# Shared expert and router of one tile in products of 256 and 320 columns, with the last projection half split around the turn

## The chip, the cores and the metric

The kernel runs on one core of one Trainium2 chip. The metric is the device time of one execution in microseconds (us); lower is better. The kernel before takes 2959.06 us, the median of three runs (2958.59 to 2960.01). TensorE is called PE in the profile, its weight loads PEld, VectorE DVE, ScalarE ACT, GpSimd POOL and SyncE, which here only issues DMAs, SP.

## The reference

One encoder layer is applied to two sequences of 1024 rows of 1024 values, in 32-bit floats. The change lies in the part that joins the end of the first sub-layer to the beginning of the second. Cut to that part, the reference is:

```python
def encoder_layer(x, c, p):
    ...                                             # u, gate1, shift2, scale2, gate2 from x and c
    # mixer(u): merged = [rms_norm(att) | rms_norm(lru)]; merged @ w_out   (1024 -> 1024)
    x = ln_affine(DN_ALPHA * x + gate1 * mixer(u, p), p['ln1_g'], p['ln1_b'])
    u = ln_plain(x) * (1.0 + scale2) + shift2
    x = ln_affine(DN_ALPHA * x + gate2 * moe(u, p), p['ln2_g'], p['ln2_b'])
    return x

def moe(u, p):
    scores = jax.nn.sigmoid(xt @ p['w_router'])     # 1024 -> 64
    ...                                             # group-limited choice of 6 of 64 experts
    routed = routed_experts(xt, idx, w, p['w_exp_in'], p['w_exp_out'])
    shared = swiglu(xt, p['w_sh_in'], p['w_sh_out'])
    return (routed + shared).reshape(B, S, D)

def swiglu(x, w_in, w_out):
    g, up = jnp.split(x @ w_in, 2, axis=-1)         # 1024 -> 2 * 256
    return (jax.nn.silu(g) * up) @ w_out            # 256 -> 1024
```

## The kernel before

The program is a row of stages: `front` (input projection, recurrence), `attention`, `mixing`, `experts`, `output`. The change is in `mixing`, which is the stage from about 987 to 1470 us of the profiled span. It works on 16 tiles of 128 rows, numbered 0 to 15; tiles 0 to 7 are the first sequence (`KT` = 8), 8 to 15 the second. Nothing schedules it: every engine has its own hand-written program, its instructions run in the order of the code, and the engines meet at semaphores.

On PE, round `i` of the loop does the projection of tile `i` and the shared expert and router of tile `i - 1`:

- `project(pL, ...)`, both halves: the recurrence's part of `w_out` for tile `i`, 8 products of 512 columns (L1434).
- `turn(i)`: waits for `u2_ready`, the normalised rows of tile `i - 1`, and transposes them, 8 products of 128 columns (L1443). ACT copies them to `uT` (L1215).
- `project(pA, ..., 0)`, the first half of the attention's part of `w_out`, 4 products of 512 columns (L1434).
- `shared_in(i)`, gate and up columns of the shared expert, 8 products of 512 columns into `pH` (L1453).
- `project(pA, ..., 1)`, the second half, 4 products of 512 columns (L1434). Its end raises `pa_mm`.
- `gated(i)`: waits for `h_ready`, transposes the 256 gated values, 2 products (L1459).
- `logits`: the router's 64 columns, 8 products of 64 columns into `pB` (L1464).
- `shared_out(i)`: 4 products of 512 columns (L1472), then `rank` (L1481, L1482), 2 products of 64 columns.

A 32-bit product is two instructions in the trace, each with its own weight load: 8 products are "x16". Such an instruction is called a pass below.

On DVE, round `i` is: `add_lru(i)` (L1255, waits for `pl_mm`); `gate(i - 1)` (L1313, waits for ACT's silu of the gate columns, L1221); `add_att(i)` (L1261, waits for `pa_mm`); `norms(i)`, which is two layer norms, `add_shared(i - 1)` (L1267) among them and L1309 as its last instruction, which raises `u2_ready`; then `ranks(i - 2)` and `router(i - 1)`, a chain of some 30 small instructions. Tile 7 has more: before `gate(6)` and after `norms(7)` DVE folds the second sequence's gate into `w_out` (`fold`, L1282, 4 + 4 instructions), whose chunks come by DMA. PE's second projection of tile 8 waits for the last of them. Rounds 0 and 2 fold the shared expert's output weights (L1274) behind `norms`.

After round 15 PE turns tile 15, makes its logits first and its shared expert after them. DVE then has ranks, router and tables left, and its list of slots is what `experts` starts from.

Of the kernel before, what the change touches and what calls it, by code (L numbers as in the profile page):

```python
# [19 lines left out]
P = 128  # L20
# [1006 lines left out]
def mixing(nc, x, mod_d, w_out, weights, shared, keep, qx, lruT, u2_d, route, left, exp_weights, apart):  # L1027
# [9 lines left out]
    with ExitStack() as ctx:  # L1037
# [3 lines left out]
        wr, wsi, wso = sb("mx_wr", [P, KD, N_EXP]), sb("mx_wsi", [P, KD, 2 * D_E]), sb("mx_wso", [P, NB, D_E // P, D])  # L1041
# [43 lines left out]
        LOG, RNK = 0, 64  # L1085
# [7 lines left out]
        ut_mm, ut_copied, h_mm, silu_ready, h_ready, ht_mm, ht_copied = (sem("ut_mm"), sem("ut_copied"), sem("h_mm"), sem("silu_ready"), sem("h_ready"),  # L1093
# [8 lines left out]
        def _(sp):  # L1102
# [15 lines left out]
            sp.dma_start(wsi[:], w_sh_in.rearrange("(k p) f -> p k f", p=P)).then_inc(w_in, 16)  # L1118
# [4 lines left out]
            for dst, src in ((wr[:], w_router), (rb[:], router_bias.partition_broadcast(P)), (iota[:], iota_d.partition_broadcast(P))):  # L1123
                sp.dma_start(dst, src).then_inc(r_in, 16)
# [81 lines left out]
        def _(act):  # L1206
# [4 lines left out]
            def turned(i):  # L1211
                act.wait_ge(ut_mm, i)
                if i > 1:
                    act.wait_ge(log_mm, i - 1)
                nc.scalar.activation(uT, pU[:].rearrange("p a (k t) -> p (a k) t", t=P), ACT.Copy).then_inc(ut_copied, 1)  # L1215

            def shared_expert(i):
                act.wait_ge(h_mm, i)
                if i > 1:
                    act.wait_ge(h_ready, i - 1)  # L1220
                nc.scalar.activation(sl[:], pH[:, 0:D_E], ACT.Silu).then_inc(silu_ready, 1)  # L1221
                act.wait_ge(ht_mm, i)
# [4 lines left out]
            def scores(i, logits):  # L1227
                act.wait_ge(log_mm, i)
# [6 lines left out]
            for i in range(1, NT):  # L1235
                turned(i)
                shared_expert(i)
                scores(i, pB[:, LOG:LOG + N_EXP])
            turned(NT)
            scores(NT, pL[:, 0, 0:N_EXP])  # L1240
            shared_expert(NT)

        @block.vector
        def _(dve):
# [66 lines left out]
            def gate(i):  # L1311
                dve.wait_ge(silu_ready, i + 1)
                nc.vector.tensor_tensor(hg[:], sl[:], pH[:, D_E:2 * D_E], ALU.mult).then_inc(h_ready, 1)  # L1313
# [115 lines left out]
        def _(pe):  # L1429
            ident, tri, ones = cst[:, 0, :], cst[:, 1, :], cst[:, 2, :]  # L1430

            def project(out, which, src, i, h):
                for j in range(GQ):
# [12 lines left out]
            def shared_in(i):  # L1446
                if i > 1:
                    pe.wait_ge(ht_copied, i - 1)
                else:
                    pe.wait_ge(w_in, 48)  # L1450
                    pe.wait_ge(r_in, 48)
                for k in range(KD):
                    m = nc.tensor.matmul(pH[:], uT[:, k, :], wsi[:, k, :], start=(k == 0), stop=(k == KD - 1))  # L1453
# [8 lines left out]
            def logits(out):  # L1462
                for k in range(KD):
                    m = nc.tensor.matmul(out, uT[:, k, :], wr[:, k, :], start=(k == 0), stop=(k == KD - 1))  # L1464
# [11 lines left out]

# [7 lines left out]
            for i in range(NT):  # L1484
# [15 lines left out]
                project(pA, 0, attT, i, 1).then_inc(pa_mm, 1)  # L1500
                if i:
                    gated(i)
                    if i > 1:
                        pe.wait_ge(ez_ready, i - 1)
                    if i > 2:
                        pe.wait_ge(slots_ready, i - 2)
# [441 lines left out]
```

## Time and profile before

| | before |
|---|---|
| time, median of 3 runs | 2959.06 us (2958.59 to 2960.01) |
| profiled execution, its own time | 2960.4 us |
| its span, from the first to the last instruction | 2958.8 us |
| PE busy | 2760.2 us, 93% of the span |
| DVE busy | 1585.5 us, 54% |
| mean granted clock of PE | 0.969 |
| tile 6 to tile 7 in `mixing`, from turn to turn | 27.36 us |

An engine's busy time over the whole span is a mean over stages with different limits. What the change touches is read in the stage itself, from the rows of one tile in order of time and from the waits written behind them: a bracket such as [2.60 <-PE mx_pA L1434] says that the engine stood idle for 2.60 us just before the instruction, and that a PE instruction of line 1434 ended the wait. Products overlap in time, so the time that one takes is read from the start of one group of them to the start of the next, not from the duration in the row, which holds the last one's way through the array as well.

### The profile page before, as it was taken

The page shows a single profiled execution, that of the slowest core. Times are in us where ns is not written, and L with a number is a line of the kernel's source. Part 1 is how long each engine was busy: PE and PEld are TensorE (multiplying, and loading weights), DVE is VectorE, ACT ScalarE, POOL GpSimd, SP SyncE. Part 2 cuts the span into 40 slices and gives each one's busy share as a digit, 9 for nine tenths or more (in the row PEclk, how much of TensorE's full clock was granted, in tenths as well). Part 3 has the DMA queues.
Part 4 walks back from the last instruction along what each step waited for, and adds up shares of the span by engine and source line. Part 5 has one row for each costly group of instructions (what it writes and reads, how often), then busy time and mean ns, then how long its engine had stood idle before and what let it go on. Part 6 is the DMA issues. An engine that isn't in the chain of part 4 may idle for free. (4 is left out here: it accounts for less than half of the span.)

```text
span 2958.8 us, 31489 instructions
## 1 busy us (share of the span) xinstructions
PE 2760.2 (93%) x9160; PEld 1327.9 (45%) x9160; DVE 1585.5 (54%) x2549; ACT 698.0 (24%) x1222; POOL 1107.1 (37%) x1150
## 2 busy tenths in 40 slices
PE   6999999899999899899679999999999999999990
PEld 3345445455555345455334444444444444444440
DVE  3477357678877377777723333333333333333335
ACT  2354354366666111111100000000000000000005
POOL 2002001100000123223446665666665666665664
PEclk9999999999999999999889999999999999999995
DMA  8531000400000311211268798986978778989646
GB/s 330 188 112 54 18 32 8 160 12 12 9 11 8 140 65 65 100 59 49 79 212 252 203 325 235 310 255 166 289 207 265 212 227 248 281 285 307 162 99 255
DMA packets 189533, 466.46 MB, mean 158 GB/s; under 512 B 22282, under 2 KB 47050, under 8 KB 188042
## 3 DMA queue, kind: packets, MB, share of 16 engines
q1 hardware_dynamic: 137770, 311.89, 29.3%
q0 software_dynamic: 51680, 153.50, 21.2%
q8 instruction: 47, 0.77, 0.1%
q14 instruction: 36, 0.29, 0.0%
HBM read 361.38 MB, written 99.75 MB: 156 GB/s over the span
## 5 line engine op out<-in xcount | busy, mean ns | idle before, releaser
L1754 PE MATMUL ex_pH<-ring,ex_xT 128*128 x2096 | 945.4, 594 | 4.9 <-DVE ex_xT L1671 2.8
L1612 POOL DMA_INDIRECT kT<-s_u,ex_gidx x532 | 599.6, 1127 | 163.8 <-issue 159.8
L1754 PEld LDWEIGHTS ex_pH<-ring,ex_xT 128*128 128x128 f32 x2096 | 388.8, 191 | 446.5 <-issue 446.5
L1771 PE MATMUL ex_pY<-qT,ex_hT 128*128 x1040 | 467.6, 592 | 0.0
L1671 DVE STREAM_TRANSPOSE ex_xT<-kT 128x1024 f32<-128x1024 f32 x132 | 164.1, 1243 | 343.1 <-DMA kT<-s_u,ex_gidx 342.8
L1771 PEld LDWEIGHTS ex_pY<-qT,ex_hT 128*128 128x128 f32 x1040 | 197.5, 190 | 248.9 <-issue 248.9
L1632 POOL DMA_INDIRECT s_acc<-ex_y,ex_sidx x130 | 211.9, 1630 | 186.7 <-DVE ex_y L1706 121.7
L1706 DVE SCALAR_TENSOR_TENSOR ex_y<-ex_pY,ex_wgt,ex_G 128x1024 f32<-128x1024 f32 x130 | 166.9, 1284 | 183.3 <-PE ex_pY L1771 158.8
L1660 ACT ACTIVATE ex_hT<-ex_pG 128x256 f32<-128x256 f32 x130 | 50.0, 384 | 870.5 <-PE ex_pG L1741 857.1
L638 PE MATMUL fr_pF<-fr_uT,fr_wf 128*128 128x512 f32 x512 | 225.0, 595 | 1.3 <-ACT fr_uT L332 1.0
L1675 DVE TENSOR_TENSOR ex_h<-ex_silu,ex_pH 128x256 f32<-128x256 f32 x131 | 54.9, 419 | 318.7 <-ACT ex_silu L1651 318.5
L1701 DVE SCALAR_TENSOR_TENSOR ex_G<-mx_mrow,ex_second 128x1024 f32<-128x1024 f32 x130 | 166.7, 1282 | 0.0
L879 DVE TENSOR_REDUCE at_top<-at_pS 128x1 f32<-128x1024 f32 x128 | 155.8, 1217 | 16.1 <-PE at_pS L961 16.0
L827 POOL TENSOR_TENSOR mx_rms<-at_var,at_half 128x32 f32<-128x32 f32 x1 | 5.4, 5428 | 422.1 <-DVE at_var L944 422.1
L836 ACT ACTIVATE at_pr<-at_pS,at_nm,head_rms 128x1024 f32<-128x1024 f32 x128 | 153.8, 1202 | 21.0 <-DVE at_nm L880 21.0
L638 PEld LDWEIGHTS fr_pF<-fr_uT,fr_wf 128*128 128x128 f32 x512 | 96.1, 190 | 121.5 <-issue 121.2
L961 PE MATMUL at_pS<-kT,qT 64*128 64x512 f32 x256 | 146.1, 652 | 2.3 <-PEq L728 2.3
L1651 ACT ACTIVATE ex_silu<-ex_pH 128x256 f32<-128x256 f32 x131 | 50.4, 384 | 411.1 <-PE ex_pH L1754 408.1
L961 PE MATMUL at_pS<-kT,qx 64*128 64x512 f32 x256 | 146.1, 652 | 0.0
L970 PE MATMUL at_pX<-mx_cst,at_pr 128*128 128x128 f32 x1024 | 138.5, 279 | 3.8 <-ACT at_pr L836 3.1
L984 PE MATMUL at_pO<-at_pT,v 128*64 128x256 f32 x1024 | 138.5, 392 | 0.6 <-DVE qT L902 0.6
L1188 POOL DMA_INDIRECT s_list<-mx_entry,mx_slots x96 | 94.8, 988 | 112.9 <-DVE mx_slots L1366 88.5
(284 smaller groups left out, 3172.9 us busy)
## 6 DMA issues: line engine op xcount, KB each, us to landing
ring<-in_w_exp_in SPq DMA_DIRECT2D x64, 2048.0 KB
qT<-in_w_exp_out SPq DMA_DIRECT2D x64, 1024.0 KB
fr_wq<-in_w_ada SPq DMA_DIRECT2D x32, 512.0 KB, 5.5
kT<-s_u,ex_gidx POOLq DMA_INDIRECT x536
fr_wf<-in_w_in SPq DMA_DIRECT2D x16, 512.0 KB, 5.7
mx_x<-in_x SPq DMA_DIRECT2D x16, 512.0 KB
s_u<-v SPq DMA_DIRECT2D x16, 512.0 KB, 2.8
s_acc<-mx_x SPq DMA_DIRECT2D x16, 512.0 KB, 2.7
```

Of the source, the lines that this page charges most:

```text
L638: m = nc.tensor.matmul(pF[:, u % 2, :], wf[:, n % 4, k, :], uT[:, k, h * 512:(h + 1) * 512], start=(k == 0), stop=(k == KD - 1))
L836: nc.scalar.activation(pr[:, n % 2, :], pS[:, n % 2, :], ACT.Exp, bias=nm[:, n % 16:n % 16 + 1], scale=head_rms(n), accum_out=rs[:, n % 16 ...
L879: step(nc.vector.tensor_reduce(top[:, n % 16:n % 16 + 1], pS[:, n % 2, :], AX.X, ALU.max, negate=True))
L961: m = nc.tensor.matmul(pS[:, n % 2, h * 512:(h + 1) * 512], q, kT[rows, b, g, :], start=True, stop=True)
L970: m = nc.tensor.transpose(pX[:, h, k * P:(k + 1) * P], pr[:, n % 2, (4 * h + k) * P:(4 * h + k + 1) * P], ident)
L1612: nc.gpsimd.indirect_dma_start(xg[:, u, g, :], None, u2_q, bass.IndirectOffsetOnAxis(ap=gidx[:, u, g:g + 1].bitcast(U32), axis=0)).then_in ...
L1632: nc.gpsimd.indirect_dma_start(acc_d, bass.IndirectOffsetOnAxis(ap=sidx[:, u:u + 1].bitcast(U32), axis=0), y[:, u, :], None, compute_op=AL ...
L1671: nc.vector.transpose(xT[:, u, :, :].rearrange("p k (g j) -> p g k j", g=4), xg[:, u, :, :].rearrange("p g (k i) -> p g k i", i=S)).then_i ...
L1701: nc.vector.scalar_tensor_tensor(G[:], g2[:, 1, :], second[:, bass.ds(b, 1)], g2[:, 0, :], ALU.mult, ALU.add).then_inc(gate_ready, 1)
L1706: nc.vector.scalar_tensor_tensor(y[:, u, :], pY[:].rearrange("p a f -> p (a f)"), wgt[:, bass.ds(b, 1)], G[:], ALU.mult, ALU.mult).then_in ...
L1754: m = nc.tensor.matmul(pH[:], xT[:, u, k, :], wi[:, bass.ds(slot, 1), k, :].rearrange("p a f -> p (a f)"), start=(k == 0), stop=(k == KD - 1))
L1771: m = nc.tensor.matmul(pY[:, h, :], hT[:, c, :], wo[:, bass.ds(slot, 1), c, h * 512:(h + 1) * 512].rearrange("p a d -> p (a d)"), start=(c ...
```

## The change

The router's 64 columns are stored behind the shared expert's 512, in one tile `mx_wsi` of 576 columns. In rounds 1 to 15 `shared_in` now makes two groups: 8 products of 256 columns (the gate columns, into `pH`, raising the new semaphore `hs_mm`), then 8 products of 320 columns (up columns and router columns together, into `pB`, raising `h_mm`). ACT's silu waits for `hs_mm`, DVE's gate now for `h_mm` as well, and reads the up columns from `pB`. The separate products of 64 columns are gone in these rounds; the last tile keeps the old form. The second projection half is cut in two: 2 products, then `gated`, then 2 products, and `pa_mm` comes behind the last.

```diff
@@ -1038,7 +1038,7 @@
         sb = lambda n, s, d=F32: ctx.enter_context(nc.sbuf_tensor(n, s, d))
         ps = lambda n, s: ctx.enter_context(nc.psum_tensor(n, s, F32))
         sem = lambda n: ctx.enter_context(nc.semaphore("mx_" + n))
-        wr, wsi, wso = sb("mx_wr", [P, KD, N_EXP]), sb("mx_wsi", [P, KD, 2 * D_E]), sb("mx_wso", [P, NB, D_E // P, D])
+        wsi, wso = sb("mx_wsi", [P, KD, 2 * D_E + N_EXP]), sb("mx_wso", [P, NB, D_E // P, D])
         rb, ln, iota, tokf = sb("mx_rb", [P, N_EXP]), sb("mx_ln", [P, 2, D]), sb("mx_iota", [P, N_EXP]), sb("mx_tokf", [P, 1])
 
         attT, stg, ut = keep[0], keep[1][:].rearrange("p b g t -> p b (g t)"), keep[2][:].rearrange("p (s n) d -> p s (n d)", s=2)
@@ -1082,7 +1082,8 @@
         pH = ps("mx_pH", [P, 512])
         pB = ps("mx_pB", [P, 512])
         R1, R2, V1, V2 = range(4)
-        LOG, RNK = 0, 64
+
+        UP, LOG, RNK = 0, D_E, D_E + N_EXP
 
         once, x_in, stg_in, wo_folded = sem("once"), [sem(f"x_in{s}") for s in range(NX)], [sem("stg_in0"), sem("stg_in1")], sem("wo_folded")
         grow_in, tokf_in, ln_in, w_in, r_in = sem("grow_in"), sem("tokf_in"), sem("ln_in"), sem("w_in"), sem("r_in")
@@ -1090,7 +1091,7 @@
         var1, rstd1, x1_ready, z_stored, var2, rstd2, u2_ready, u2_stored = (
             sem("var1"), sem("rstd1"), sem("x1_ready"), [sem(f"z_stored{s}") for s in range(NX)], sem("var2"), sem("rstd2"), sem("u2_ready"),
             [sem("u2_stored0"), sem("u2_stored1")])
-        ut_mm, ut_copied, h_mm, silu_ready, h_ready, ht_mm, ht_copied = (sem("ut_mm"), sem("ut_copied"), sem("h_mm"), sem("silu_ready"), sem("h_ready"),
+        ut_mm, ut_copied, hs_mm, h_mm, silu_ready, h_ready, ht_mm, ht_copied = (sem("ut_mm"), sem("ut_copied"), sem("hs_mm"), sem("h_mm"), sem("silu_ready"), sem("h_ready"),
                                                                         sem("ht_mm"), sem("ht_copied"))
         log_mm, ez_ready, y_mm, z_ready, g2_in, wso_folded = sem("log_mm"), sem("ez_ready"), sem("y_mm"), sem("z_ready"), sem("g2_in"), sem("wso_folded")
         m_ready, rank_mm, slots_ready, listed = sem("m_ready"), sem("rank_mm"), sem("slots_ready"), [sem("listed0"), sem("listed1")]
@@ -1115,12 +1116,12 @@
             load_x(0)
             sp.dma_start(ln[:], ln1_rows.partition_broadcast(P)).then_inc(ln_in, 16)
             load_x(1)
-            sp.dma_start(wsi[:], w_sh_in.rearrange("(k p) f -> p k f", p=P)).then_inc(w_in, 16)
+            sp.dma_start(wsi[:, :, 0:2 * D_E], w_sh_in.rearrange("(k p) f -> p k f", p=P)).then_inc(w_in, 16)
             gate2 = lambda b: mod_d[b:b + 1, 5 * D:6 * D].partition_broadcast(P)
             for b in range(NB):
                 sp.dma_start(wso[:, b, :, :], w_sh_out.rearrange("(c p) d -> p c d", p=P)).then_inc(w_in, 16)
             sp.dma_start(g2[:], gate2(0)).then_inc(g2_in, 16)
-            for dst, src in ((wr[:], w_router), (rb[:], router_bias.partition_broadcast(P)), (iota[:], iota_d.partition_broadcast(P))):
+            for dst, src in ((wsi[:, :, 2 * D_E:], w_router), (rb[:], router_bias.partition_broadcast(P)), (iota[:], iota_d.partition_broadcast(P))):
                 sp.dma_start(dst, src).then_inc(r_in, 16)
             load_x(2)
             sp.dma_start(grow[:], mod_d[1:2, 2 * D:3 * D].partition_broadcast(P)).then_inc(grow_in, 16)
@@ -1211,21 +1212,26 @@
             def turned(i):
                 act.wait_ge(ut_mm, i)
                 if i > 1:
-                    act.wait_ge(log_mm, i - 1)
+                    act.wait_ge(h_mm, i - 1)
                 nc.scalar.activation(uT, pU[:].rearrange("p a (k t) -> p (a k) t", t=P), ACT.Copy).then_inc(ut_copied, 1)
 
-            def shared_expert(i):
-                act.wait_ge(h_mm, i)
+            def silu(i):
+                act.wait_ge(hs_mm, i)
                 if i > 1:
                     act.wait_ge(h_ready, i - 1)
                 nc.scalar.activation(sl[:], pH[:, 0:D_E], ACT.Silu).then_inc(silu_ready, 1)
+
+            def gated_rows(i):
                 act.wait_ge(ht_mm, i)
                 if i > 1:
                     act.wait_ge(y_mm, i - 1)
                 nc.scalar.activation(hT[:], pH[:, 0:FC * P].rearrange("p (c t) -> p c t", t=P), ACT.Copy).then_inc(ht_copied, 1)
 
             def scores(i, logits):
-                act.wait_ge(log_mm, i)
+                if i < NT:
+                    act.wait_ge(h_mm, i)
+                else:
+                    act.wait_ge(log_mm, 1)
                 if i > 2:
                     act.wait_ge(m_ready, i - 2)
                 nc.scalar.activation(ez[:, i % 2, :], logits, ACT.Exp, scale=-1.0).then_inc(ez_ready, 1)
@@ -1234,11 +1240,13 @@
             silu_table()
             for i in range(1, NT):
                 turned(i)
-                shared_expert(i)
+                silu(i)
+                gated_rows(i)
                 scores(i, pB[:, LOG:LOG + N_EXP])
             turned(NT)
             scores(NT, pL[:, 0, 0:N_EXP])
-            shared_expert(NT)
+            silu(NT)
+            gated_rows(NT)
 
         @block.vector
         def _(dve):
@@ -1310,7 +1318,12 @@
 
             def gate(i):
                 dve.wait_ge(silu_ready, i + 1)
-                nc.vector.tensor_tensor(hg[:], sl[:], pH[:, D_E:2 * D_E], ALU.mult).then_inc(h_ready, 1)
+
+                up = pH[:, D_E:2 * D_E]
+                if i < NT - 1:
+                    dve.wait_ge(h_mm, i + 1)
+                    up = pB[:, UP:UP + D_E]
+                nc.vector.tensor_tensor(hg[:], sl[:], up, ALU.mult).then_inc(h_ready, 1)
 
             def router(i):
                 by_rank = lambda a, n: a.unsqueeze(1).to_broadcast([P, n, a.shape[1]])
@@ -1429,8 +1442,8 @@
         def _(pe):
             ident, tri, ones = cst[:, 0, :], cst[:, 1, :], cst[:, 2, :]
 
-            def project(out, which, src, i, h):
-                for j in range(GQ):
+            def project(out, which, src, i, h, j0=0, j1=GQ):
+                for j in range(j0, j1):
                     m = nc.tensor.matmul(out[:, h, :], src[:, j, i * P:(i + 1) * P], wo[:, which, j, h * 512:(h + 1) * 512],
                                          start=(j == 0), stop=(j == GQ - 1))
                 return m
@@ -1449,8 +1462,20 @@
                 else:
                     pe.wait_ge(w_in, 48)
                     pe.wait_ge(r_in, 48)
+                first = D_E if i < NT else 2 * D_E
                 for k in range(KD):
-                    m = nc.tensor.matmul(pH[:], uT[:, k, :], wsi[:, k, :], start=(k == 0), stop=(k == KD - 1))
+                    m = nc.tensor.matmul(pH[:, 0:first], uT[:, k, :], wsi[:, k, 0:first], start=(k == 0), stop=(k == KD - 1))
+                m.then_inc(hs_mm, 1)
+                if i == NT:
+                    return
+
+                if i > 1:
+                    pe.wait_ge(ez_ready, i - 1)
+                    pe.wait_ge(h_ready, i - 1)
+                if i > 2:
+                    pe.wait_ge(slots_ready, i - 2)
+                for k in range(KD):
+                    m = nc.tensor.matmul(pB[:, 0:D_E + N_EXP], uT[:, k, :], wsi[:, k, D_E:], start=(k == 0), stop=(k == KD - 1))
                 m.then_inc(h_mm, 1)
 
             def gated(i):
@@ -1461,7 +1486,7 @@
 
             def logits(out):
                 for k in range(KD):
-                    m = nc.tensor.matmul(out, uT[:, k, :], wr[:, k, :], start=(k == 0), stop=(k == KD - 1))
+                    m = nc.tensor.matmul(out, uT[:, k, :], wsi[:, k, 2 * D_E:], start=(k == 0), stop=(k == KD - 1))
                 m.then_inc(log_mm, 1)
 
             def shared_out(i):
@@ -1473,7 +1498,6 @@
                 m.then_inc(y_mm, 1)
 
             def rank(i, read):
-
                 pe.wait_ge(m_ready, i)
                 pe.wait_ge(ez_ready, read)
                 if i > 1:
@@ -1497,14 +1521,11 @@
                 if i:
                     pe.wait_ge(ut_copied, i)
                     shared_in(i)
-                project(pA, 0, attT, i, 1).then_inc(pa_mm, 1)
+                project(pA, 0, attT, i, 1, 0, GQ // 2)
                 if i:
                     gated(i)
-                    if i > 1:
-                        pe.wait_ge(ez_ready, i - 1)
-                    if i > 2:
-                        pe.wait_ge(slots_ready, i - 2)
-                    logits(pB[:, LOG:LOG + N_EXP])
+                project(pA, 0, attT, i, 1, GQ // 2, GQ).then_inc(pa_mm, 1)
+                if i:
                     shared_out(i)
                 if i >= 2:
                     rank(i - 1, i)
```

PE's rows in one whole round of the loop before, which is alike in rounds 3 to 15: `mx_pL` and `mx_pA` are the two projections, `mx_pU` is first the turn and then the shared expert's output, `mx_pH` the shared expert's input columns and then the turned gated values, `mx_pB` the logits and the ranks.

```order
L1434 MATMUL mx_pL<-ring 128x512 x8
L1443 MATMUL mx_pU<-mx_cst,v 128x128 x8
L1434 MATMUL mx_pA<-ring,qT 128x512 x4
L1453 MATMUL mx_pH<-mx_wsi,qx 128x512 x8
L1434 MATMUL mx_pA<-ring,qT 128x512 x4
L1459 MATMUL mx_pH<-mx_cst,mx_h 128x128 x2
L1464 MATMUL mx_pB<-mx_wr,qx 128x64 x8
L1472 MATMUL mx_pU<-mx_wso,mx_hT 128x512 x4
L1481 MATMUL mx_pB<-mx_M,mx_cst 128x64
L1482 MATMUL mx_pB<-mx_Msum,mx_cst 128x64
```

The same round now:

```order
L1447 MATMUL mx_pL<-ring 128x512 x8
L1456 MATMUL mx_pU<-mx_cst,v 128x128 x8
L1447 MATMUL mx_pA<-ring,qT 128x512 x4
L1467 MATMUL mx_pH<-mx_wsi,qx 128x256 x8
L1478 MATMUL mx_pB<-mx_wsi,qx 128x320 x8
L1447 MATMUL mx_pA<-ring,qT 128x512 x2
L1484 MATMUL mx_pH<-mx_cst,mx_h 128x128 x2
L1447 MATMUL mx_pA<-ring,qT 128x512 x2
L1497 MATMUL mx_pU<-mx_wso,mx_hT 128x512 x4
L1505 MATMUL mx_pB<-mx_M,mx_cst 128x64
L1506 MATMUL mx_pB<-mx_Msum,mx_cst 128x64
```

The 8 rows of 64 columns behind `mx_h`'s turn are gone, the 8 of 512 columns into `mx_pH` are 8 of 256 and 8 of 320, and two of the four products into `mx_pA` now stand behind the two of `mx_h`. Between the round's turn and the last product into `mx_pA` stood 4 + 8 + 4 products; now it is 4 + 16 + 2 + 2 + 2.

On DVE no instruction moves. What the gate reads changes, and what it waits for. DVE's first rows of a round before:

```order
L1255 SCALAR_TENSOR_TENSOR mx_x<-mx_pL,mx_rms,mx_x 128x1024
L1313 TENSOR_TENSOR mx_h<-mx_silu,mx_pH 128x256
L1261 SCALAR_TENSOR_TENSOR mx_x<-mx_pA,mx_rms,mx_x 128x1024
L1286 BN_STATS mx_st<-mx_x 128x6 x2
L1289 BN_AGGR mx_mv<-mx_st 128x2
L1290 TENSOR_SCALAR mx_sm<-mx_mv 128x1
```

And now:

```order
L1263 SCALAR_TENSOR_TENSOR mx_x<-mx_pL,mx_rms,mx_x 128x1024
L1326 TENSOR_TENSOR mx_h<-mx_silu,mx_pB 128x256
L1269 SCALAR_TENSOR_TENSOR mx_x<-mx_pA,mx_rms,mx_x 128x1024
L1294 BN_STATS mx_st<-mx_x 128x6 x2
L1297 BN_AGGR mx_mv<-mx_st 128x2
L1298 TENSOR_SCALAR mx_sm<-mx_mv 128x1
```

The gate stands where it stood, ahead of `add_att`.

## Rows read from the trace of the kernel before

**Rows 1.** Busy us in a stretch: PE, PEld, DVE, ACT, POOL; clock, DMA, GB/s

```profile
1130.00:1160.00 30.00, 30.00 (x93) 15.02 (x92) 23.90 (x62) 4.79 (x7) 10.88 (x11) 1.00 0.15 53
```

**Rows 2.** Timeline, PE, one round: start, us, line, tiles, count, idle before

```profile
1151.43 1.04 PE L1443 MATMUL mx_pU<-mx_cst,v 128*128 128x128 f32 x8
...
1155.74 7.03 PE L1453 MATMUL mx_pH<-mx_wsi,qx 128*128 128x512 f32 x16
1162.61 3.60 PE L1434 MATMUL mx_pA<-ring,qT 128*128 128x512 f32 x8
1166.04 0.38 PE L1459 MATMUL mx_pH<-mx_cst,mx_h 128*128 128x128 f32 x2
1166.26 1.90 PE L1464 MATMUL mx_pB<-mx_wr,qx 128*128 128x64 f32 x16
1167.99 3.65 PE L1472 MATMUL mx_pU<-mx_wso,mx_hT 128*128 128x512 f32 x8
...
1178.79 1.04 PE L1443 MATMUL mx_pU<-mx_cst,v 128*128 128x128 f32 x8
```

**Rows 3.** Timeline, DVE, same round

```profile
1163.22 0.42 DVE L1313 TENSOR_TENSOR mx_h<-mx_silu,mx_pH 128x256 f32<-128x256 f32 x1 [0.99 <-ACT mx_silu L1221]
1166.24 1.28 DVE L1261 SCALAR_TENSOR_TENSOR mx_x<-mx_pA,mx_rms,mx_x 128x1024 f32<-128x1024 f32 x1 [2.60 <-PE mx_pA L1434]
...
1176.65 1.28 DVE L1309 SCALAR_TENSOR_TENSOR v<-v,mx_sm,mx_mrow 128x1024 f32<-128x1024 f32 x1
```

**Rows 4.** Timeline, PE and DVE, turn of round 1

```profile
1011.98 1.28 DVE L1309 SCALAR_TENSOR_TENSOR v<-v,mx_sm,mx_mrow 128x1024 f32<-128x1024 f32 x1 [0.52 <-POOL mx_sm L1182]
...
1013.32 1.59 PE L1443 MATMUL mx_pU<-mx_cst,v 128*128 128x128 f32 x8 [4.23 <-DVE v L1309]
```

**Rows 5.** Timeline, PE, products of 256 columns in an earlier stage

```profile
299.62 3.62 PE L657 MATMUL fr_pK<-fr_wq,fr_uT 128*128 128x256 f32 x16
303.08 7.03 PE L638 MATMUL fr_pF<-fr_uT,fr_wf 128*128 128x512 f32 x16
```

**Rows 6.** Timeline, DVE, rounds 1 to 3

```profile
1029.87 1.28 DVE L1261 SCALAR_TENSOR_TENSOR mx_x<-mx_pA,mx_rms,mx_x 128x1024 f32<-128x1024 f32 x1 [2.60 <-PE mx_pA L1434]
...
1067.36 1.28 DVE L1309 SCALAR_TENSOR_TENSOR v<-v,mx_sm,mx_mrow 128x1024 f32<-128x1024 f32 x1
...
1082.29 0.41 DVE L1313 TENSOR_TENSOR mx_h<-mx_silu,mx_pH 128x256 f32<-128x256 f32 x1
```

**Rows 7.** Timeline, DVE, tiles 7 and 8

```profile
1197.97 1.28 DVE L1261 SCALAR_TENSOR_TENSOR mx_x<-mx_pA,mx_rms,mx_x 128x1024 f32<-128x1024 f32 x1
...
1234.46 1.28 DVE L1261 SCALAR_TENSOR_TENSOR mx_x<-mx_pA,mx_rms,mx_x 128x1024 f32<-128x1024 f32 x1 [2.60 <-PE mx_pA L1434]
```

**Rows 8.** Timeline, PE, tiles 7 and 8

```profile
1198.11 0.69 PE L1459 MATMUL mx_pH<-mx_cst,mx_h 128*128 128x128 f32 x2 [4.55 <-DVE mx_h L1313]
...
1218.95 5.17 PE L1434 MATMUL mx_pA<-ring,qT 128*128 128x512 f32 x8 [3.71 <-DVE ring L1282]
1223.96 7.03 PE L1453 MATMUL mx_pH<-mx_wsi,qx 128*128 128x512 f32 x16
```

**Rows 9.** Stretches, columns as in rows 1: after two waits of PE

```profile
1198.00:1205.00 7.00, 6.89 (x22) 5.25 (x23) 6.22 (x10) 3.38 (x5) 1.54 (x1) 0.51 0.32 111
170.00:180.00 10.00, 8.74 (x22) 3.61 (x21) 9.86 (x7) 4.53 (x6) 0.00 (x0) 1.00 0.77 312
```

**Rows 10.** Timeline, PE, the wait inside the second of them

```profile
176.85 1.98 PE L679 MATMUL fr_pG<-fr_xc,fr_wg 128*128 128x512 f32 x4 [1.26 <-ACT qT L390]
```

**Rows 11.** Timeline, DVE, tile 15 and the last wait for PE

```profile
1426.00 1.28 DVE L1261 SCALAR_TENSOR_TENSOR mx_x<-mx_pA,mx_rms,mx_x 128x1024 f32<-128x1024 f32 x1 [2.60 <-PE mx_pA L1434]
...
1465.33 1.22 DVE L1267 SCALAR_TENSOR_TENSOR mx_x<-mx_x,mx_pU 128x1024 f32<-128x1024 f32 x1 [0.36 <-PE mx_pU L1472]
```

**Rows 12.** Router and its tables: DMA issues of line 1124

```profile
L1124 SPq DMA_DIRECT2D mx_wr<-in_w_router x1: 973/973/973, 994.7 to 994.7; - x1
...
DMA to landing us min/median/max: 12.7/13.3/13.4
```

## The prediction

> **What bounds the kernel now.** I first read the table of stretches. In a middle stretch of `mixing` PE works through: 30.00 of 30.00 us, clock 1.00, while DVE has 23.90 [rows 1]. That looks like a stage that gains whatever PE is spared. The timeline of one round qualifies it. From turn to turn it takes 27.36 us [rows 2], and the same round on DVE [rows 3] closes a ring: PE turns a tile, makes projection half, shared expert and second half, DVE takes the result up in `add_att`, runs the norms, and L1309 hands the next tile to the next turn. The two legs:
>
> - turn (1151.43) to `add_att` (1166.24): 14.81 us [rows 2, 3].
> - `add_att` to the end of L1309 (1176.65 + 1.28 = 1177.93): 11.69 us, all of it `norms` [rows 3].
> - from there to a turn on a PE that stands waiting: 1013.32 - (1011.98 + 1.28) = 0.06 us [rows 4].
>
> The ring is 26.56 us, PE's own row of work 27.36: PE leads by only 0.80 us. Logits, `shared_out`, ranks and the next `pL` projection lie outside the ring, behind `pa_mm`. The reader should see that work spared there pays for 0.80 us at most, and that work added before `pa_mm` lengthens the ring. DVE's 2.60 us wait ahead of `add_att` [rows 3] shows that PE gives the start of its leg.
>
> **The columns.** Removed: 16 passes of 512 columns, 1155.74 to 1162.61, 6.87 us; and 16 of 64 columns, 1166.26 to 1167.99, 1.73 us [rows 2]. Added: 16 passes of 256 columns, which in an earlier stage, also against 128 x 128 weights, took 299.62 to 303.08, 3.46 us [rows 5]; and 16 of 320 columns, which no row has. 512 columns cost 1.99 times as much as 256, so the price goes by columns: from 256 upwards 3.46 x 320/256 = 4.33, from 512 downwards 6.87 x 320/512 = 4.29. I take 4.31, on the line through both; the ends differ by 0.04. In the freest reading 16 passes of 320 lie between 3.46 and 6.87, but a cost that jumps between two proportional ones has nothing in the rows for it. Sum 7.77. PE is spared 6.87 + 1.73 - 7.77 = 0.83 us a round, and needs 26.53. But in the ring only the 6.87 stood; now 7.77 stand there: +0.90.
>
> **The split half.** The two passes of the gated turn cost 1166.26 - 1166.04 = 0.22 us [rows 2] and now come before `pa_mm`: another +0.22. Together the leg grows by 1.12, and the ring to 26.56 + 1.12 = 27.68 us. That is above PE's 26.53, so the ring sets the round: +0.32 on 27.36, PE standing 1.15 us ahead of each turn.
>
> Does DVE's gate, which now also waits for the 320-column group, delay PE? It comes after the turn by (1155.74 - 1151.43) + 7.77 + 0.20 = 12.28 us (0.20 is 1166.04 to 1166.24, PE to DVE [rows 2, 3]), takes 0.42 [rows 3], and PE wants the result at 4.31 + 7.77 + 1.72 = 13.80 (1.72 is half of 3.43, the old second half). Covered by 1.1 us. Behind the gate on DVE stands only `add_att`, later anyway. The silu comes earlier than before, the copy to `hT` has the last 1.72 us of projection as cover where it had 1.73 us of logits, and the scores have `shared_out`. These cost nothing. In round 3 DVE comes late, having folded after round 2: the gate ends at 1082.70, 14.06 us after L1309's end at 1068.64 [rows 6]. PE wants it 13.86 us after that end and gets it at 14.12: 0.26 once.
>
> **Tile 7.** This is the second large term. Before, `gate(6)` came late, behind four folds: PE stood 4.55 us before the gated turn at 1198.11 [rows 8]. `add_att(7)` did not mind: its projection was ready, and it started at 1197.97 [rows 7]. Now half of that projection stands behind the gated turn. PE restarts at the lower clock: 1198 to 1205 has 0.51, the 1.2 GHz level [rows 9]. So 0.44 for the turn (twice 0.22), 3.44 for four passes (twice 4 x 6.87/16), 0.20 to DVE: 1198.11 + 4.08 = 1202.19 against 1197.97, +4.22. What follows (norms, folds 4 to 7, the projection of tile 8 at 1218.95 after a wait for the fold [rows 8]) hangs on DVE and shifts whole. At the full clock the step would be 2.28.
>
> **The sum.** In times of `add_att` [rows 6, 3, 7, 11]:
>
> - tile 1: +1.12 (PE's path from a turn that DVE gives already).
> - tiles 1 to 6: 5 x 27.68 = 138.40 against 1166.24 - 1029.87 = 136.37, +2.03, and +0.26.
> - tile 7: +4.22. Tile 8: +1.12.
> - tiles 8 to 15: 7 x 27.68 = 193.76 against 1426.00 - 1234.46 = 191.54, +2.22.
>
> Together +10.97. After `add_att(15)` DVE's chain of norms, ranks and router sets the end; the last tile is made as before, and the only wait for PE near the end is 0.36 us [rows 11]. `experts` starts from this chain's list, so the shift goes through whole. The router's load now writes pieces of 256 bytes into wider rows: issued at 994.7, landed after 13.3 [rows 12], so by 1008; PE's shared expert first needs it 4.31 us and more after 1013.32. A margin of some 10 us: nothing, or, if it took twice as long, at most 3 us once. It isn't below nothing, since nobody waits for it today.
>
> The profiled execution took 2960.4 us (span 2958.8 and 1.6 around it); +11.0 gives 2971.4. The median of the runs is 1.3 below that execution, so the forecast is **2970** us. This case's own range: tile 7 at full clock takes 1.9 off; tile 8, where PE now waits about 4 us longer for the fold, can restart slower: its first four products took 5.01 us against 3.43 at full clock [rows 8, 2], 6.86 would be all of it at the lower clock, +1.9; the ring by 0.05 either way over twelve rounds is 0.6: 2967 to 2974.
>
> **A rule that speaks against it.** After 1.26 us of waiting PE went on at clock 1.00 in 170 to 180 us [rows 9, 10]; after 4.55 us it ran at 0.51 [rows 9]. The Trainium skill, "TensorE: Matmul & The Clock Gate", section "A second HAM failure mode: psum-queue depth-cycling", says that a kernel whose PE idles briefly between groups of products often enough can have its clock swing between the two levels and lose throughput. By that rule the 1.15 us in every round could cost the clock. The trace so far is against it, at that length of wait.
>
> **The rivals.**
> - *PE is the bound and gets its 0.83 us a round.* Faster. It decides if the ring has more than 1.95 us (1.12 + 0.83) of room instead of 0.80: DVE's leg would have to be 10.5 us and not 11.69. Thirteen rounds (tiles 2 to 6 and 8 to 15) give -10.8: 2948. For it: PE at 30.00 of 30.00. Against: both legs, read above.
> - *Tile 7 hides the step.* If PE's gated turn there isn't held as in rows 8, or the time returns in the waits for folded chunks (DVE waits for DMAs there too), 4.22 drop out: 2966. Against: the chunk loads are issued after DVE's own folds and move with them.
> - *The clock falls in the new waits.* Each round then loses what tile 8 lost, 5.01 - 3.43 = 1.58 us; over twelve rounds 19 more: 2989.
> - *The change does not act in the ring*, for instance since waits that the trace doesn't show pace DVE: within 2 us of before.
>
> **How the numbers follow.** Forecast 0.80, tile 7 hidden 0.09, PE the bound 0.04, clock 0.03, no action 0.04. What a measurement can tell from no change is 0.2%, 5.9 us, so slower begins at 2965.0. Faster 0.04; same 0.04 and a third of the hidden tile 7, 0.07; slower 0.89. The range reaches from 2963 to 2976, over the hidden tile 7 and the router's load.
>
> **What would show it.** Right: turn to turn 27.7 us in the steady rounds; a wait of about 1.1 us before each turn, ended by DVE's last norm instruction; DVE's wait ahead of `add_att` longer than 2.60; the two groups of the shared expert at 3.46 and 4.31 us; at tile 7 `add_att` held for four products behind a late gated turn; `add_att(15)` 11 us later, and as much at the start of `experts`. Wrong: rounds of 26.5 us with PE still at 30 of 30; a 320-column group well off 4.31; clock below 1 in steady rounds; or a tail after tile 15 of another length.

## The result, and the profile after

The changed kernel takes 2970.26 us (median of 6 runs, 2967.20 to 2971.42) against 2958.72 for the kernel before on the same chip: ratio 1.0037, 95% interval 1.0026 to 1.0048. It is slower by 11.5 us. A repetition on another occasion gave 2970.08 against 2958.67, 1.0041 (1.0028 to 1.0055). The profiled execution took 2967.2 us, span 2965.6, 3 us below its median: its first projection of `mixing` starts at 983.95 us, and 986.65 in the profile before, ahead of all that the change touches. `add_att(0)` is 2.76 us earlier in it too, `add_att(15)` 8.17 later. `experts` makes its first product 71.78 us after `add_att(15)`, 71.62 before, so the stage passes its loss on whole; the rest of the span is 1.5 us shorter, 1459.65 against 1461.18. Together this is the 6.8 us between the two spans.

The stretch that answers to [rows 1]: PE no longer works through, though its clock is full.

```profile
1130.00:1160.00 30.00, 28.97 (x97) 16.86 (x97) 23.42 (x61) 5.17 (x8) 10.77 (x10) 1.00 0.16 53
```

One round on PE, the answer to [rows 2]:

```profile
1151.02 1.09 PE L1456 MATMUL mx_pU<-mx_cst,v 128*128 128x128 f32 x8 [1.03 <-DVE v L1317]
1151.95 3.60 PE L1447 MATMUL mx_pA<-ring,qT 128*128 128x512 f32 x8
1155.39 3.62 PE L1467 MATMUL mx_pH<-mx_wsi,qx 128*128 128x256 f32 x16
1158.84 4.47 PE L1478 MATMUL mx_pB<-mx_wsi,qx 128*128 128x320 f32 x16
1163.15 1.88 PE L1447 MATMUL mx_pA<-ring,qT 128*128 128x512 f32 x4
1164.86 0.38 PE L1484 MATMUL mx_pH<-mx_cst,mx_h 128*128 128x128 f32 x2
1165.08 1.88 PE L1447 MATMUL mx_pA<-ring,qT 128*128 128x512 f32 x4
1166.80 3.60 PE L1497 MATMUL mx_pU<-mx_wso,mx_hT 128*128 128x512 f32 x8
...
1170.62 7.09 PE L1447 MATMUL mx_pL<-ring 128*128 128x512 f32 x16
1178.74 1.09 PE L1456 MATMUL mx_pU<-mx_cst,v 128*128 128x128 f32 x8 [1.03 <-DVE v L1317]
```

From turn to turn 27.72 us. The gate columns take 3.45 us, up and router columns 4.31, and PE stands 1.03 us ahead of the turn, until DVE's last norm instruction. Over rounds 2 to 15 this wait is 1.01 to 1.43 us, mostly 1.03. The same round on DVE, the answer to [rows 3]: the wait for the projection is 3.16 us where it was 2.60, and the row 1177.41 ends just before PE's turn at 1178.74.

```profile
1163.42 0.42 DVE L1326 TENSOR_TENSOR mx_h<-mx_silu,mx_pB 128x256 f32<-128x256 f32 x1 [0.79 <-PE mx_pB L1478]
1167.00 1.28 DVE L1269 SCALAR_TENSOR_TENSOR mx_x<-mx_pA,mx_rms,mx_x 128x1024 f32<-128x1024 f32 x1 [3.16 <-PE mx_pA L1447]
...
1177.41 1.28 DVE L1317 SCALAR_TENSOR_TENSOR v<-v,mx_sm,mx_mrow 128x1024 f32<-128x1024 f32 x1
```

Tile 7, the answer to [rows 7, 8]. PE waits 6.46 us for the late gate, and `add_att` then waits 3.65 us for the four passes behind the gated turn. It did not wait at all before. The folds' own waits for their chunks come to 7.0 us against 7.3: 3.52 against 3.13 ahead of the late gate, 3.45 against 4.19 behind `norms(7)`.

```profile
1198.74 0.41 DVE L1326 TENSOR_TENSOR mx_h<-mx_silu,mx_pB 128x256 f32<-128x256 f32 x1
1202.81 1.28 DVE L1269 SCALAR_TENSOR_TENSOR mx_x<-mx_pA,mx_rms,mx_x 128x1024 f32<-128x1024 f32 x1 [3.65 <-PE mx_pA L1447]
...
1239.62 1.28 DVE L1269 SCALAR_TENSOR_TENSOR mx_x<-mx_pA,mx_rms,mx_x 128x1024 f32<-128x1024 f32 x1 [3.16 <-PE mx_pA L1447]
...
1199.21 0.69 PE L1484 MATMUL mx_pH<-mx_cst,mx_h 128*128 128x128 f32 x2 [6.46 <-DVE mx_h L1326]
1199.69 3.08 PE L1447 MATMUL mx_pA<-ring,qT 128*128 128x512 f32 x4
1202.61 3.60 PE L1497 MATMUL mx_pU<-mx_wso,mx_hT 128*128 128x512 f32 x8
...
1223.04 5.13 PE L1447 MATMUL mx_pA<-ring,qT 128*128 128x512 f32 x8 [7.40 <-DVE ring L1290]
1228.01 3.62 PE L1467 MATMUL mx_pH<-mx_wsi,qx 128*128 128x256 f32 x16
...
1198.00:1203.00 5.00, 3.79 (x7) 1.88 (x8) 1.35 (x3) 3.01 (x4) 0.00 (x0) 0.59 0.63 196
```

The end of the stage, the answer to [rows 11], keeps its shape: DVE's last wait for PE is 0.38 us.

```profile
1434.17 1.28 DVE L1269 SCALAR_TENSOR_TENSOR mx_x<-mx_pA,mx_rms,mx_x 128x1024 f32<-128x1024 f32 x1 [3.16 <-PE mx_pA L1447]
...
1473.51 1.22 DVE L1275 SCALAR_TENSOR_TENSOR mx_x<-mx_x,mx_pU 128x1024 f32<-128x1024 f32 x1 [0.38 <-PE mx_pU L1497]
```

Term by term, in distances between the starts of `add_att`:

| from tile to tile | before | after | measured | predicted |
|---|---|---|---|---|
| 0 to 1 | 27.61 | 28.72 | +1.11 | +1.12 |
| 1 to 6 | 136.37 | 138.78 | +2.41 | +2.29 |
| 6 to 7 | 31.73 | 35.81 | +4.08 | +4.22 |
| 7 to 8 | 36.49 | 36.81 | +0.32 | +1.12 |
| 8 to 15 | 191.54 | 194.55 | +3.01 | +2.22 |
| sum | 423.74 | 434.67 | +10.93 | +10.97 |

### The profile page after: what moved, and what is told of

The parts are those of the page before. It is cut to its first block and busy times, and to the rows that moved or that the text cites. A ratio compares the mean times of both kernels' runs of the same rounds, so it can differ in the third digit from the quotient of the medians.

```text
span 2965.6 us, 31505 instructions
## 1 busy us (share of the span) xinstructions
PE 2745.2 (93%) x9160; PEld 1340.3 (45%) x9160; DVE 1585.1 (53%) x2549; ACT 697.2 (24%) x1222; POOL 1098.5 (37%) x1150
## 5 line engine op out<-in xcount | busy, mean ns | idle before, releaser
L1633 POOL DMA_INDIRECT kT<-s_u,ex_gidx x532 | 592.3, 1113 | 163.8 <-issue 158.7
```

What stands on the lines that cost most here:

```text
L1633: nc.gpsimd.indirect_dma_start(xg[:, u, g, :], None, u2_q, bass.IndirectOffsetOnAxis(ap=gidx[:, u, g:g + 1].bitcast(U32), axis=0)).then_in ...
```

## The experiments

Each ratio is to the kernel before on the same chip, over 3 or 5 rounds, with its 95% interval. The theory is the ring: turn, projection, shared expert, `add_att`, norms, next turn. Its two legs can be read in every profile: "leg" below is the time from turn to `add_att`.

### The two halves of the change apart

```diff
-                project(pA, 0, attT, i, 1, 0, GQ // 2)
+                project(pA, 0, attT, i, 1).then_inc(pa_mm, 1)
                 if i:
                     gated(i)
-                project(pA, 0, attT, i, 1, GQ // 2, GQ).then_inc(pa_mm, 1)
-                if i:
                     shared_out(i)
```

> The changed kernel with the second projection half whole again, ahead of the gated turn; the products of 256 and 320 columns stay. Ring theory: the leg from turn to add_att grows by 0.90 us (7.77 for 6.87), the ring to 27.46, 0.10 above the 27.36 of before. Sum: tile 1 +0.90, tiles 1 to 6 5 x 27.46 - 136.37 = +0.93, tile 7 nothing (add_att again has its projection before the late gate), tile 8 +0.90, tiles 8 to 15 7 x 27.46 - 191.54 = +0.68: +3.4 us on the kernel before. Rival 1, PE is the bound and the wider products cost what they should: -0.83 a round, -11 us. Rival 2, all of the loss comes with the new products (more of them on PE, two PSUM banks): the full +11.5 stays.

Measured: 2962.79 against 2959.05 us, 1.0011 (1.0002 to 1.0020), +3.7 us. The leg is 15.76 us in every steady round, the round 27.50. It also shows what the split was good for:

```profile
1331.76 1.09 PE L1456 MATMUL mx_pU<-mx_cst,v 128*128 128x128 f32 x8 [0.24 <-DVE v L1317]
...
1343.88 3.60 PE L1447 MATMUL mx_pA<-ring,qT 128*128 128x512 f32 x8
1347.32 0.38 PE L1484 MATMUL mx_pH<-mx_cst,mx_h 128*128 128x128 f32 x2
1348.17 3.70 PE L1497 MATMUL mx_pU<-mx_wso,mx_hT 128*128 128x512 f32 x8 [0.47 <-ACT mx_hT L1228]
```

Without the 64-column products or half a projection behind it, the gated turn is followed by 0.47 us in which PE waits for ACT's copy. From the gated turn's start to the shared output are 0.85 us instead of 0.22. Here that lies outside the ring and costs nothing. The turn at 1331.76 follows norms of 11.85 us; in the steady rounds no wait is written before the turn, which starts 0.05 to 0.06 us after DVE's last norm instruction all the same.

The other half alone, on the kernel before:

```diff
-                project(pA, 0, attT, i, 1).then_inc(pa_mm, 1)
+                project(pA, 0, attT, i, 1, 0, GQ // 2)
+                if i:
+                    gated(i)
+                project(pA, 0, attT, i, 1, GQ // 2, GQ).then_inc(pa_mm, 1)
                 if i:
-                    gated(i)
```

> The kernel before with the second projection half split around the gated turn, products of 512 and 64 columns as they were. Ring theory: the ring is 26.56 + 0.22 = 26.78, still below PE's 27.36, so no steady round changes; tile 7 pays about 4.1 us, since half of its projection now stands behind a gated turn that comes late, and the last tile 0.2: +4.3 us on the kernel before, all of it in the one interval from tile 6 to tile 7. Rival, the split is free everywhere (the loss is in the columns): 0.

Measured: 2963.21 against 2959.05 us, 1.0014 (1.0005 to 1.0023), +4.2 us. The leg is 15.03 us, the steady round still 27.36, and tile 6 to tile 7 takes 35.42 us instead of 31.73. That interval had been expected to hold all of the cost; but round 3, in which DVE's gate comes late, is 0.79 us longer than its neighbours too. Here PE's gated turn and the four passes behind the folds:

```profile
1198.30 0.69 PE L1459 MATMUL mx_pH<-mx_cst,mx_h 128*128 128x128 f32 x2 [6.45 <-DVE mx_h L1313]
1198.78 3.07 PE L1434 MATMUL mx_pA<-ring,qT 128*128 128x512 f32 x4
1201.69 1.89 PE L1464 MATMUL mx_pB<-mx_wr,qx 128*128 128x64 f32 x16
```

The legs add up: 14.81 before, +0.95 with the columns, +0.22 with the split, 15.98 with both. The times don't: 3.7 + 4.2 = 7.9 of 11.5 us. Most of the rest is PE's lead of 0.80 us: the split alone stays inside it, the columns alone pass it by 0.14 us a round, both by 0.36, which is 2.6 us over twelve rounds. The times of the halves are no finer than that: each interval reaches 2.7 us to either side, and in the two profiles tile 7 to tile 8 took 38.34 and 38.23 us instead of 36.49, a spread that the next runs show.

### Tile 7

```diff
-                project(pA, 0, attT, i, 1, 0, GQ // 2)
+                split = GQ if i == KT - 1 else GQ // 2
+                m = project(pA, 0, attT, i, 1, 0, split)
+                if split == GQ:
+                    m.then_inc(pa_mm, 1)
                 if i:
                     gated(i)
-                project(pA, 0, attT, i, 1, GQ // 2, GQ).then_inc(pa_mm, 1)
+                if split < GQ:
+                    project(pA, 0, attT, i, 1, split, GQ).then_inc(pa_mm, 1)
```

> The changed kernel, but in round 7 alone the second projection half is whole and ahead of the gated turn. Ring theory: the interval from tile 6 to tile 7 falls back from 35.8 to 31.7 us, steady rounds stay at 27.7: 4.1 us less than the changed kernel, about 7.3 above the kernel before. Rival, the fold waits for its chunks and gives nothing back: same as the changed kernel.

Measured: 2968.07 us, 1.0027 (1.0016 to 1.0038), only 2 us below the changed kernel. Tile 6 to tile 7 did come back to 31.62 us, but tile 7 to tile 8 took 39.46 instead of 36.81. So I ran both once more, side by side:

> The changed kernel once more, unaltered, to stand on the same chip beside the version that is whole in round 7: 2970, 11 us above the kernel before.

> The version that is whole in round 7 once more. In its first profile the interval from tile 6 to tile 7 came back by 4.2 us, but the one from tile 7 to tile 8 grew by 2.65, of which 1.6 was a projection half at the lower clock for longer (6.57 us for 8 passes where the changed kernel's took 4.97). If that was the clock's chance, this run gives 3 to 4 us against the changed kernel on the same chip; if it belongs to the version, again about 2.

Measured: 2970.08 for the changed kernel and 2966.17 for this one, 1.0041 (1.0028 to 1.0055) and 1.0025 (1.0015 to 1.0035): 3.9 us apart, near the 4.1 of the term. The two intervals overlap, the runs hardly do (2968.48 to 2973.06, and 2963.60 to 2968.71). Now it was the changed kernel that took 39.16 us from tile 7 to tile 8, and this one 36.87. Two things vary between profiles of the same kernel, both after `norms(7)`: from its last instruction to the first product of tile 8, with the folds and their chunks between, 8.46 to 9.67 us in four profiles of these two kernels; and the row of tile 8's first four products, behind PE's wait, 5.13 to 6.73. The changed kernel's second profile at tiles 7 and 8, and this version's second:

```profile
1200.41 0.69 PE L1484 MATMUL mx_pH<-mx_cst,mx_h 128*128 128x128 f32 x2 [6.05 <-DVE mx_h L1326]
1200.89 3.23 PE L1447 MATMUL mx_pA<-ring,qT 128*128 128x512 f32 x4
...
1225.52 6.34 PE L1447 MATMUL mx_pA<-ring,qT 128*128 128x512 f32 x8 [8.52 <-DVE ring L1290]
```

```profile
1199.67 0.69 PE L1484 MATMUL mx_pH<-mx_cst,mx_h 128*128 128x128 f32 x2 [4.64 <-DVE mx_h L1326]
...
1219.66 5.28 PE L1447 MATMUL mx_pA<-ring,qT 128*128 128x512 f32 x8 [4.47 <-DVE ring L1290]
```

### The ring made longer by a known piece

In `norms`, on the kernel before and on the changed one, the same instruction is issued twice:

```diff
                 step(nc.vector.scalar_tensor_tensor(u, z, mv[:, 1, 0:1], mrow[:, i // KT, 1, :], ALU.subtract, ALU.mult))
+                step(nc.vector.scalar_tensor_tensor(u, z, mv[:, 1, 0:1], mrow[:, i // KT, 1, :], ALU.subtract, ALU.mult))
```

> The kernel before, with the centring of u in norms done twice (the same 1.28 us instruction writes the same values again): 1.3 us more on DVE between add_att and the next turn. PE's work is untouched. Ring theory: the ring is 26.56 + 1.3 = 27.86, so steady rounds grow from 27.36 to about 27.86, not by 1.3: PE's lead of 0.80 swallows the rest. 12 rounds x 0.5, and the full 1.3 at tile 1, 7, 8 and in the tail: about +11 us. Rival, PE is the bound and DVE has 6 us to spare in a round: steady rounds stay 27.36, +5 at most.

Measured: 2971.22 against 2958.82 us, 1.0042 (1.0027 to 1.0056), +12.4. Norms grow by 1.32 us, the round by 0.57, to 27.93, and PE now waits 0.32 to 0.75 us ahead of every steady turn, mostly 0.35, in a kernel whose PE work is untouched:

```profile
1366.89 1.09 PE L1444 MATMUL mx_pU<-mx_cst,v 128*128 128x128 f32 x8 [0.35 <-DVE v L1310]
```

> The changed kernel, with the same instruction doubled. Ring theory: the ring sets every round there, so each grows by the whole 1.3 us, to 29.0: 16 x 1.3 = +21 us on the changed kernel, about 2991. Rival, PE is the bound with some added cost of its own products: PE's wait of 1.15 ahead of the turn isn't a limit, +10 or less.

Measured: 3010.28 us, 1.0174 (1.0160 to 1.0189), +40 on the changed kernel where the ring alone gives 21. This is a miss of both theories. Rounds take 30.7 us, not 29.0:

```profile
1274.42 1.09 PE L1457 MATMUL mx_pU<-mx_cst,v 128*128 128x128 f32 x8 [2.35 <-DVE v L1318]
...
1334.44 1.97 PE L1457 MATMUL mx_pU<-mx_cst,v 128*128 128x128 f32 x8 [2.35 <-DVE v L1318]
1336.20 4.40 PE L1448 MATMUL mx_pA<-ring,qT 128*128 128x512 f32 x8
1340.43 3.62 PE L1468 MATMUL mx_pH<-mx_wsi,qx 128*128 128x256 f32 x16
...
1330.00:1360.00 30.00, 27.65 (x85) 15.79 (x84) 21.90 (x57) 4.79 (x7) 8.41 (x8) 0.94 0.16 53
1334.44:1336.20 1.76, 1.76 (x8) 1.76 (x9) 1.61 (x6) 0.00 (x0) 0.00 (x0) 0.50 1.02 407
```

The wait ahead of the turn is 2.35 us, and the turn and the first products after it run at the lower level: turn 1.76 us instead of 0.93, at a granted clock of 0.50, and four products 4.23 instead of 3.44. The leg grows by up to 1.68 us, inside the ring. The stretch has a granted clock of 0.94. So it goes in twelve rounds, with waits of 2.33 to 2.76 us; in one, the turn at 1274.42, the clock held after 2.35 us, and the leg stayed at 15.98. Sixteen times 1.32 us are 21, the longer legs of eleven rounds outside tiles 7 and 8 are 17.9: 39 of the 40. It is the rival that the prediction had given 0.03, called up by a longer wait. Half the piece (the first 512 columns once more) asks where it begins:

> The changed kernel, with the centring of the first 512 columns of u done once more ahead of the whole (about 0.7 us on DVE). With a full one PE's wait before each turn was 2.35 us, the granted clock 0.94, and the leg from turn to add_att 17.65 us instead of 15.98. Here the wait is between the changed kernel's 1.2 and that, about 1.8. If the clock holds at this wait: leg 15.98, rounds of 28.4, 16 x 0.7 = +11 on the changed kernel, about 2981. If it falls in every round: leg 17.65, rounds of 30.1, some 22 more, about 3003.

Measured: 2986.24 us, 1.0094 (1.0079 to 1.0110), +16 on the changed kernel, between the two. Eleven rounds have a wait of 1.80 to 1.82 us and the clock 1.00 behind it, with a leg of 15.98 (16.26 in round 3). In two, tile 1 to 2 and tile 9 to 10, the wait was longer, 2.23 and 2.17 us, since PE has no ranks to make yet ahead of the first, and norms took 12.83 us and not 12.48 ahead of the second; there the clock fell behind the turn, and the leg is 17.68:

```profile
1291.73 1.17 PE L1457 MATMUL mx_pU<-mx_cst,v 128*128 128x128 f32 x8 [2.17 <-DVE v L1318]
1292.70 5.26 PE L1448 MATMUL mx_pA<-ring,qT 128*128 128x512 f32 x8
1297.80 3.62 PE L1468 MATMUL mx_pH<-mx_wsi,qx 128*128 128x256 f32 x16
...
1321.94 1.09 PE L1457 MATMUL mx_pU<-mx_cst,v 128*128 128x128 f32 x8 [1.82 <-DVE v L1318]
...
1288.00:1300.00 12.00, 9.83 (x31) 5.40 (x30) 10.65 (x37) 1.02 (x1) 4.11 (x5) 0.86 0.38 132
1330.00:1360.00 30.00, 28.18 (x93) 16.11 (x92) 23.51 (x59) 5.13 (x8) 9.55 (x10) 1.00 0.16 54
```

Sixteen rounds of 0.79 us are 12.6, two slow legs 3.4: together the 16.

### The shared expert taken out of the ring

```diff
@@ DVE, in norms(i), ahead of the second statistics
+                if i and i != KT - 1:
+                    gate(i - 1)
                 stats(z, 1, EPS, V2, var2)
@@ DVE's loop
-                if i:
+                if i == KT - 1:
                     gate(i - 1)
                 add_att(i)
@@ PE's loop
+            def ahead(i):
+                return 2 if 0 < i < NT - 1 and i != KT - 1 else 0
...
-                if i:
+                begun = ahead(i - 1)
+                if i and not begun:
                     pe.wait_ge(l_added, i)
...
-                project(pL, 1, lruT, i, 0)
+                project(pL, 1, lruT, i, 0, begun, GQ)
...
                 project(pA, 0, attT, i, 0)
+                project(pA, 0, attT, i, 1).then_inc(pa_mm, 1)
                 if i:
                     pe.wait_ge(ut_copied, i)
                     shared_in(i)
-                project(pA, 0, attT, i, 1, 0, GQ // 2)
-                if i:
+                    if ahead(i):
+                        pe.wait_ge(l_added, i + 1)
+                        project(pL, 1, lruT, i + 1, 0, 0, ahead(i))
                     gated(i)
-                project(pA, 0, attT, i, 1, GQ // 2, GQ).then_inc(pa_mm, 1)
-                if i:
                     shared_out(i)
```

> The changed kernel's products in an order that takes the shared expert out of the ring: turn, whole attention projection (raises pa_mm 7.94 us after the turn instead of 15.9), products of 256 and 320 columns, two products of the next tile's pL as cover, gated turn, shared output, ranks, rest of pL; on DVE the gate stands inside norms, ahead of the second statistics, except in round 7, which keeps its order. Ring theory: PE is the bound again with 26.53 us a round, 0.83 less than before; tail and tile 7 also start 3 us earlier relative to their turn, since DVE is done earlier: 13 rounds x -0.83, -3.1 before tile 7 and -3.1 at the end, -16 us, about 2943. DVE's own row is about 26.5 us in such a round, so it can come out up to 0.5 a round worse: 2943 to 2950. Rival, the new products themselves cost the time: no faster than the kernel before.

Measured: 2951.34 us against 2959.05, 0.9974 (0.9964 to 0.9983). Faster by 7.7 us with the changed kernel's products, so the products were not what cost; but the time misses the expected 2943 to 2950, as rounds took 27.2 us instead of 26.53. PE's rows show where:

```profile
1342.53 1.88 PE L1449 MATMUL mx_pL<-ring 128*128 128x512 f32 x4
1344.24 0.38 PE L1486 MATMUL mx_pH<-mx_cst,mx_h 128*128 128x128 f32 x2
1345.10 3.70 PE L1499 MATMUL mx_pU<-mx_wso,mx_hT 128*128 128x512 f32 x8 [0.47 <-ACT mx_hT L1228]
```

It is the copy again, 0.64 us a round, and now PE is the bound, so it counts. A third product of the next tile's `pL` now goes ahead, behind the gated turn:

```diff
-                return 2 if 0 < i < NT - 1 and i != KT - 1 else 0
+                return 3 if 0 < i < NT - 1 and i != KT - 1 else 0
...
-                        project(pL, 1, lruT, i + 1, 0, 0, ahead(i))
+                        project(pL, 1, lruT, i + 1, 0, 0, 2)
                     gated(i)
+                    if ahead(i):
+                        project(pL, 1, lruT, i + 1, 0, 2, 3)
```

> As the version with the projection first, but a third product of the next tile's pL now stands between the gated turn and the shared output. In that version's trace PE stood 0.64 us a round there, waiting for ACT's copy of the turned values (gated turn to shared output 0.86 us, of which 0.22 is the turn): rounds came out at 27.2 instead of 26.53. Theory: PE is the bound there, so the cover brings each of the 12 covered rounds to 26.5-26.6: -7.7 us on that version, about 2943.6. Rival, DVE is the bound in that version (its row of a round is about 26.5 us with its waits): within 2 us of that version, and DVE without a wait ahead of add_shared.

Measured: 2945.36 us against 2958.82, 0.9956 (0.9942 to 0.9970): 13.5 us less than the kernel before, and 25 less than the changed one. Steady rounds take 26.47 us from turn to turn, the leg is mostly 9.73, and PE works through again. Ten such rounds, each 0.89 us below the 27.36 of before, give 8.9 of the 13.5 us, and 2.95 are won between the last two turns:

```profile
1320.81 1.04 PE L1458 MATMUL mx_pU<-mx_cst,v 128*128 128x128 f32 x8
...
1336.31 1.88 PE L1449 MATMUL mx_pL<-ring 128*128 128x512 f32 x4
1338.03 0.38 PE L1486 MATMUL mx_pH<-mx_cst,mx_h 128*128 128x128 f32 x2
1338.25 1.02 PE L1449 MATMUL mx_pL<-ring 128*128 128x512 f32 x2
1339.11 3.60 PE L1499 MATMUL mx_pU<-mx_wso,mx_hT 128*128 128x512 f32 x8
...
1310.00:1340.00 30.00, 30.00 (x98) 16.69 (x97) 24.59 (x62) 6.32 (x9) 8.96 (x9) 1.00 0.16 53
```

> The version with the projection first and the copy covered, with the full extra instruction (1.3 us) in norms. Theory: there DVE waits about 2 us in norms for the shared expert's output anyway, and PE is the bound, so steady rounds stay at 26.5; the 1.3 us is paid at tile 0 and in tiles 7 and 8, where DVE's folds set the time, at most +5 us: 2945 to 2950. Rival, DVE's chain is what sets the round in that version too: +1.3 a round, +20.

Measured: 2947.84 us, 0.9961 (0.9948 to 0.9974), within the intervals of the version without the piece. Steady rounds stay at 26.5 us. The same instruction cost 12.4 us in the kernel before, 40 in the changed one and 2.5 here, which is not clear of noise.

## Why the prediction was right

- **What bounds the kernel.** The ring with PE 0.80 us ahead. Shown: the extra piece of 1.32 us lengthens a round before by 0.57, that is by all but 0.75 (the 0.80, less 0.05 that comes below), with PE's work untouched. PE's own row is 26.47 us where it sets the round with the same products (predicted 26.53).
- **The columns.** 320 columns at 4.31 us, as taken from the line through 256 and 512. +0.90 predicted, +0.95 read in the leg. The 0.05 is the turn: on a PE that stands waiting, the next group starts 0.93 us after it and not 0.87, which I had read from a PE at work. The same 0.05 makes the round 27.72 instead of 27.68.
- **The split.** +0.22 predicted, and +0.22 in the leg with and without the other half. DVE's gate, behind its new wait (0.79 us), holds up no steady round; round 3 is 0.24 longer than its neighbours, 0.26 was predicted. The split alone, without PE's wait ahead of the turn, pays 0.79 there.
- **Tile 7.** +4.22 predicted, +4.08 in the profile, +3.69 with the split alone, 3.9 us in the side-by-side runs. The first figure hides two misses. The four passes took 2.92 us and not 3.44, as the clock came back before their end, so that the step from PE's late turn to `add_att` is 3.60 us and not 4.08. But the late turn itself came 0.34 us later after `add_att(6)` than before, as the folds ahead of the gate waited 0.39 us longer for their chunks, which the prediction had not in its sum.
- **Tile 8 and the last tiles.** +1.12 and +2.22 predicted, +0.32 and +3.01 in the profile, which is the weakest part of the agreement. In this profile the folds behind `norms(7)` waited 0.74 us less for their chunks than before, which the prediction did not have either. The differences of -0.80 here and +0.79 on the last tiles cancel, and that the sum of this profile comes within 0.04 us of the forecast is luck. From tile 7 to tile 8 the same kernel took 36.81 us in one profile and 39.16 in another, half of it PE's restart (the prediction had a spread of 1.9 us for it) and half the folds' chunks, for which it had none. The excess on the last tiles is 7 x 0.05 and two rounds in which norms took 11.85 and 12.04 us instead of 11.68. They stand at the same two tiles, 11 and 13, in six profiles; in the two of the changed kernel with a lengthened ring one longer row of norms stands at tile 9. Why is open.
- **The clock.** At waits of 1.01 to 1.43 us ahead of the turn PE kept its clock through the turn in rounds 2 to 15, as the prediction said from the 1.26 us of [rows 10]. What it did not say is how near the edge lies: in the lengthened rings the clock held at 1.80 to 1.82 us in eleven rounds, fell at 2.17 and 2.23, and from 2.33 to 2.76 fell in twelve rounds and held in one. By the Trainium skill, "TensorE: Matmul & The Clock Gate", section "A second HAM failure mode: psum-queue depth-cycling", short idling between groups of products can make the clock swing. The changed kernel's rows don't show that, those of the lengthened ring do.
- **The rivals.** PE as the bound is ruled out by the two lengthened kernels. A fold that swallows tile 7's step is ruled out by the 3.9 us of the side-by-side runs. A change that does not act in the ring is ruled out by the legs. The router's load into wider rows shows no cost: issued at 991.42 us, it landed 14.1 us later, ahead of the shared expert's first products at 1016.61, and tile 0 to tile 1 grew by 1.11 us, all of it the ring's.

## What to carry to other kernels

An engine that is busy all of a stretch is not yet its bound by more than its lead over the next ring: add up the ring of waits through the other engine, and the difference is all that can be won by sparing the busy one. Work saved behind the point that the other engine waits for is worth no more than the lead, and work added ahead of it costs in full once the lead is used up (here 1.17 us in the leg, 0.36 a round), so first ask on which side of that point a product stands. The same products gained 13.5 us here as soon as the projection that DVE waits for went ahead of them, with a piece of other work on either side of the small turn that ACT has to copy.

## What the hardware showed beyond expectation

- A wait of PE in each round has a second price: 0.79 us more of DVE work cost 16 us over sixteen rounds, 1.32 us more cost 40. Up to 1.82 us of waiting ahead of the turn the clock was full in every steady round, in the two rounds with 2.17 and 2.23 us it fell to the 1.2 GHz level behind the turn (granted 0.50), and with about 2.35 us it was down from the turn's start (0.94 in the stretch, up to 1.68 us more per round), in all rounds but one.
- A turn that starts on a waiting PE takes 0.93 us to the next group, one on a working PE 0.87.
- After the same wait at tile 8, PE's first four products took 4.97 us (1223.04 to 1228.01) in one profile of the changed kernel; in its second one, after 8.52 us of waiting and not 7.40, the row is 6.34 us long where it was 5.13.
